# Expert weight pieces in eight lasting places, output weights by column halves, two modulation pieces multiplied ahead of their layer

## The chip, the cores and the metric

One NeuronCore of a Trainium2 chip runs the whole program. The metric is the device time of one execution in microseconds (us). Five engines run side by side and meet through semaphores: TensorE (PE, matmuls), VectorE (DVE), ScalarE (ACT), GpSimd (POOL) and SyncE (SP), whose queue issues nearly all transfers from HBM.

## What is computed

The reference chains a two-layer transformer block with experts and a second, hybrid block. The change touches the first alone. Per layer (512 tokens of width 1024, all float32):

```python
mod = c_act @ w_ada[l] + b_ada[l]                     # 6 x 1024 modulation values
h = rms_norm(x, norm1_g[l]) * (1.0 + scale1) + shift1
proj = h @ w_in[l]                                    # latents, rope part, convolution input
attn_out, conv_out = mla_group(...), conv_group(...)
x = x + gate1 * (concatenate([attn_out, conv_out]) @ w_out[l])
h2 = rms_norm(x, norm2_g[l]) * (1.0 + scale2) + shift2
# 16 experts; each takes the 64 tokens with the highest affinity
hid = silu(xe @ w_gate) * (xe @ w_up)
ye = (hid @ w_down) * gate
x = x + gate2 * scatter(ye)
```

Each expert has three 1024 x 1024 matrices, 12.6 MB, for 64 tokens.

## The kernel before, in words

`prologue` loads x and the constants, turns x, computes the rope tables and stores them to HBM, and issues the loads of the first layer's vector rows (13 small ones) and of modulation pieces 0 to 3. It is a block of its own: all engines meet at its end, before `layer` begins. `layer` is one such block, run twice in a loop over `l`.

Inside `layer` each engine has its own instruction stream; the order of transfers is the order of SP's stream, and a wait in it holds back all that stands behind.

**Start of a layer.** w_ada comes in twelve pieces of 512 columns (2 MB each, `ADA_PLACES` says in which of four places). PE multiplies a piece in `ada_chunk` (L541), 64 matmul records, ACT copies the row out (`ada_kept`, L909), PE turns it (`ada_turn`, L547). Pieces 0 to 3 hold shift1 and scale1, which `h` needs. Piece 0 is followed by the broadcast of 1/rms (L519), from which DVE makes the normalized x (L1101, eight operations); then come pieces 1, 2 and 3, DVE's sum `modulation(0)` (L1107), ACT's h (L933), DVE's low half of the split (L1143) and the first matmul of the input projection (L567). SP begins the layer with the first four tiles of w_in (`load_input`, L147).

**Output weights.** w_out (4 MB) lies in ring parts 3 and 4, split by ACT (L1007) and POOL (L491) during the attention into a high and a low part that are stored in parts 3, 4, 5 and in `one_hot_T`. `out_passes` (L689 to L691) multiplies them, output tile after output tile, and counts `wout_done` up to 8.

**Experts.** The weights of an expert come in six pieces of 2 MB: gate 0, 1, up 2, 3, down 4, 5. There are six lasting places in `ring`, and three `early` places that expert 1's pieces 0 to 2 use once. In `sp`: pieces 0 to 2 of expert 0 are issued when the attention is done, pieces 3 to 5 and the three early ones when all of w_out is used. From then on each piece is issued when PE has used the one that was in its place (`chunk_used`). PE's loop runs over pairs of experts: gate and up (L829), gather for the next expert (L792), turns (L838, L798), gates and a row of ranks (L804, L805), down (L851); every second expert is followed by the scatter of a pair's outputs (L814, L817), which DVE adds into x (L1318). The last pair is scattered behind the loop, where PE first waits for ACT (L1059) and POOL (L497) to split the outputs.

The issue order of the weights of expert e in the loop is

```python
def shifted(e, j):
    sp.wait_ge(chunk_used, 6 * e + (j - 5))
    load(e, j)
```

that is, pieces in the order of their use, each released six pieces ahead of its use. In the first layer the loop's tail loads modulation pieces 0 to 3 of the next layer, in the second the memory and the first weights of the next block (`load_mixer`).

## Time and profile before

| | |
|---|---|
| median of 3 runs | 2645.95 us (2644.2 to 2647.7) |
| the profiled execution | 2650.9 us, its span 2649.2 us |
| PE busy | 2484.0 us, 94% of the span |
| DVE, ACT, POOL busy | 1109.6, 871.3, 294.7 us |
| read from HBM | 641.99 MB |
| layer 0, first matmul of the input projection | at 46.84 us |
| layer 0, experts | from 335.67 to 805.5 us |
| layer 1, experts | from 1130.92 to about 1599.9 us |

Times in a timeline count from the start of the span. The span is one execution, 5 us longer than the median of the runs. Busy matmul time has modelled ends, so a busy PE can still be a PE that waits a little. The idle time in front of an instruction stands in brackets, with what ended it. A transfer has two times: how long SP was held by its issue, and how long it took from issue to landing.

### The profile page before, as it was taken

What the parts mean: (1) busy time and instruction counts of PE and PEld (TensorE: products, weight loads), DVE (VectorE), ACT (ScalarE), POOL (GpSimd) and SP (SyncE); (2) the same over time, 40 slices, a digit from 0 to 9 for tenths busy, and PEclk for the clock granted to TensorE, in tenths of its full rate; (3) what the DMA queues carried; (4) which work ended last, traced back from release to release, by engine and by line L of the source; (5) the groups of instructions that cost most, each with busy time, mean ns of one, the idle gap of its engine ahead of it and who ended that gap; (6) DMA issues with size and microseconds to landing.
All of it is one profiled execution on the core that took longest, in us unless ns stands there. A gap on an engine that the chain in (4) does not pass through costs nothing. (4 is left out here: it accounts for less than half of the span.)

```text
span 2649.2 us, 31866 instructions
## 1 busy us (share of the span) xinstructions
PE 2484.0 (94%) x12913; PEld 1487.9 (56%) x12913; DVE 1109.6 (42%) x1700; ACT 871.3 (33%) x1195; POOL 294.7 (11%) x126
## 2 busy tenths in 40 slices
PE   6989799999997989799999998999999999989998
PEld 5834533333335834533333337887788777756665
DVE  4974322222223974322222225647521112456765
ACT  4246111111114247111111116556532234245553
POOL 0002000000000002000000005000244423200000
PEclk8988899999998988899999999999999999989999
DMA  9700579999999600589999996532223321159995
GB/s 339 275 1 37 221 307 409 410 410 410 410 409 346 244 1 34 221 321 409 410 410 410 410 409 191 168 93 81 79 75 97 131 71 57 48 177 373 358 354 208
DMA packets 276596, 650.49 MB, mean 246 GB/s; under 512 B 12144, under 2 KB 110718, under 8 KB 276222
## 3 DMA queue, kind: packets, MB, share of 16 engines
q1 hardware_dynamic: 273310, 638.87, 64.2%
q0 software_dynamic: 2592, 7.87, 0.8%
q10 hardware_dynamic: 576, 2.10, 0.2%
q8 instruction: 84, 1.38, 0.2%
q14 instruction: 34, 0.28, 0.0%
HBM read 641.99 MB, written 8.39 MB: 246 GB/s over the span
## 5 line engine op out<-in xcount | busy, mean ns | idle before, releaser
L829 PE MATMUL ps<-ring,scr 128*64 128x512 f32 x1952 | 425.3, 593 | 0.8 <-DMA ring<-in_w_up 0.8
L829 PEld LDWEIGHTS ps<-ring,scr 128*64 128x64 f32 x1952 | 138.7, 137 | 277.2 <-issue 274.0
L851 PE MATMUL ps<-ring,scr 128*64 128x512 f32 x1024 | 231.9, 606 | 1.4 <-ACT scr L1047 1.4
L1579 POOL TENSOR_TENSOR raw_r<-raw,w_high 128x2048 fp32r<-128x2048 f32 (+1 forms) x38 | 165.3, 4359 | 460.0 <-ACT w_high L1846 460.0
L1601 PE MATMUL ps<-x_high,w_high 128*128 128x512 f32 x464 | 186.6, 402 | 5.4 <-DVE y L2242 5.4
L1603 PE MATMUL ps<-x_high,raw_r 128*128 128x512 f32 x464 | 184.3, 397 | 0.0
L1602 PE MATMUL ps<-xT_r,w_high 128*128 128x512 f32 x464 | 182.9, 394 | 0.0
L1123 DVE SCALAR_TENSOR_TENSOR one_hot_T<-h_tok,convw,one_hot_T 128x512 f32<-128x512 f32 x240 | 170.5, 763 | 1.8
L497 POOL TENSOR_TENSOR one_hot_T_r<-hy,one_hot_T_r 128x1024 fp32r<-128x1024 f32 x16 | 38.5, 2405 | 1124.0 <-ACT one_hot_T_r L1059 1124.0
L1331 DVE TENSOR_TENSOR scr<-scr,ps 128x512 f32<-128x512 f32 x32 | 22.0, 688 | 312.5 <-PE ps L829 312.5
L2720 DVE TENSOR_TENSOR ring_r<-ring,ring_high 128x2048 fp32r<-128x2048 f32 x56 | 127.6, 2286 | 58.4 <-ACT ring_high L2598 57.9
L851 PEld LDWEIGHTS ps<-ring,scr 128*64 128x64 f32 x1024 | 71.9, 139 | 138.7 <-issue 136.6
L1055 ACT ACTIVATE hy<-ps,gcol 64x512 f32<-64x512 f32 x64 | 43.7, 683 | 285.6 <-PE ps L851 285.2
L1846 ACT ACTIVATE w_high<-raw 128x2048 fp32r<-128x2048 f32 (+1 forms) x58 | 105.9, 1826 | 93.3 <-DMA raw<-in_p_b 49.2
L1318 DVE SCALAR_TENSOR_TENSOR xT<-ps,mod,xT 128x512 f32<-128x512 f32 x128 | 86.5, 744 | 117.3 <-PE ps L817 116.6
L1038 ACT ACTIVATE hy<-ps 128x512 f32<-128x512 f32 x32 | 19.1, 597 | 330.8 <-PE ps L792 330.8
L2598 ACT ACTIVATE ring_high<-ring 128x2048 fp32r<-128x2048 f32 x56 | 107.4, 1917 | 60.5 <-DMA ring<-in_w_up 60.5
L792 PE MATMUL ps<-h_tok,scr 128*64 128x512 f32 x512 | 120.3, 613 | 3.0 <-DVE sel_e L1302 3.0
L2511 PE MATMUL ps<-ring_high,xg_high 128*128 128x512 f32 x224 | 100.8, 450 | 3.5 <-DVE xg_low L2726 3.2
L2545 PE MATMUL ps<-ring,hidT 128*128 128x512 f32 x224 | 101.0, 593 | 2.6 <-ACT hidT L2608 2.6
L1601 PEld LDWEIGHTS ps<-x_high,w_high 128*128 128x128 f32 x464 | 87.6, 189 | 27.3 <-DVE y L2242 5.9
L1311 DVE TENSOR_TENSOR scr<-ps,smod 128x512 f32<-128x512 f32 x32 | 22.1, 692 | 187.3 <-PE ps L798 187.3
(563 smaller groups left out, 4536.2 us busy)
## 6 DMA issues: line engine op xcount, KB each, us to landing
ring<-in_w_down SPq DMA_DIRECT2D x64, 2048.0 KB, 15.2
ring<-in_w_up SPq DMA_DIRECT2D x62, 2048.0 KB, 18.4
ring<-in_w_gate SPq DMA_DIRECT2D x60, 2048.0 KB, 14.9
ring<-in_w_up SPq DMA_DIRECT2D x56, 1024.0 KB, 7.2
ring<-in_w_ada SPq DMA_DIRECT2D x22, 2048.0 KB, 13.2
ring<-in_w_down SPq DMA_DIRECT2D x28, 1024.0 KB, 7.7
raw<-in_w_in SPq DMA_DIRECT2D x24, 1024.0 KB, 5.1
raw<-in_w_in SPq DMA_DIRECT2D x20, 512.0 KB, 5.3
```

The source lines that it names most:

```text
L792: mm = pe.matmul(ps[CAP * half:CAP * (half + 1), 0, :], s_e[:, t, 0:CAP], h_tok3[:, t, half * HALF:(half + 1) * HALF], start=(t == 0), sto ...
L829: mm = pe.matmul(ps[CAP * half:CAP * (half + 1), 1 + j // 2, :], x_e[:, at_x:at_x + CAP], weights[:, k, half * HALF:(half + 1) * HALF], st ...
L851: mm = pe.matmul(ps[CAP * half:CAP * (half + 1), 4, :], hidT[:, at_f:at_f + CAP], weights[:, k, half * HALF:(half + 1) * HALF], start=(j = ...
L1123: op = dve.scalar_tensor_tensor(acc[:, c, :], src, w, acc[:, c, :], ALU.mult, ALU.add)
L1579: pool.tensor_tensor(dst, src, high.bitcast(F32), ALU.subtract).then_inc(w_ready, 1)
L1601: pe.matmul(out, s_high, m_high, start=(n == 0), stop=False)
L1602: pe.matmul(out, s_high, m_low, start=False, stop=False)
L1603: mm = pe.matmul(out, s_low, m_high, start=False, stop=(n == len(terms) - 1))
L1846: act.activation(slot_of(w_high, n), landed_chunk(n), ACT.Copy).then_inc(w_split, 1)
L2545: mm = pe.matmul(ps[:, 2 + half, :], hT[n % 2][:, k, :], w[:, k, half * HALF:(half + 1) * HALF], start=(e == 0 and k == 0), stop=(e == PER ...
L2598: act.activation(high[q], raw[q], ACT.Copy).then_inc(w_split, 1)
L2720: dve.tensor_tensor(low[q], raw[q], high[q].bitcast(F32), ALU.subtract).then_inc(w_ready, 1)
```

## The change

Four things change, all in the first block.

**Pieces.** There are eight lasting places: the six in the ring, and two (`odd`) in `hy` and `one_hot_T` that hold pieces 0 and 1 of the odd experts. Ring places 0 and 1 hold pieces 0 and 1 of the even experts, ring places 2 to 5 pieces 2 to 5 of every expert. A ninth place (`once`) holds piece 2 of expert 1. SP's order in the loop is now, for each expert: pieces 0 and 1 of the *next* expert (`following`), then pieces 2 to 5 of this one (`rest`).

**Output weights.** w_out is loaded, split and multiplied by column halves, not by row halves, so that half of its room is free at `wout_done` 4. The nine first pieces are issued in four steps instead of two: at the end of the attention, when the last of `mix` is split, at `wout_done` 4 and at 8.

**Modulation.** Pieces 0 and 1 of a layer are multiplied before the layer's block begins (`ada_ahead`, into bank 7): those of layer 0 at the end of the prologue, those of layer 1 in the tail of layer 0, in front of the last scatter. `load_input` moves from the start of the layer to the prologue and to the tail of layer 0 as well.

**Ranks.** The selector `sel_e` and a second copy of the ranks (`rank_row`, one more DVE operation) are float32r, so that L805 is a one-pass matmul.

```diff
+def ada_ahead(pe, M, c):
+    for kt in range(KT):
+        for g in range(4):
+            pe.matmul(M["ps"][GROUP * g:GROUP * (g + 1), 7, c * P:(c + 1) * P], c_spread_ahead(M)[:, kt, :], ada_place(M, ADA_PLACES[c])[:, kt, g * P:(g + 1) * P],
+                      start=(kt == 0), stop=(kt == KT - 1))
...
             for c in range(4):
                 load_ada(sp, A, M, 0, c, ahead)
+            load_input(sp, A, M, 0, ahead)
             sp.wait_ge(p_act, 2)
             sp.dma_start(A["rope"], tables).then_inc(ahead["tables"], 16)
...
+            pe.wait_ge(x_kept, KT)
+            pe.wait_ge(p_spread, 1)
+            for c in range(ADA_PRE):
+                pe.wait_ge(ahead["ada"][c], 16)
+                ada_ahead(pe, M, c)
...
-    chunk = [ring[:, i * CHUNK:(i + 1) * CHUNK].rearrange("p (k n) -> p k n", k=4) for i in range(6)]
-
-    early = [x[:, a:a + CHUNK].rearrange("p (k n) -> p k n", k=4) for x, a in ((hy, CHUNK), (one_hot_T, CHUNK), (one_hot_T, 0))]
-    EARLY = len(early)
+    chunk = [ring[:, i * CHUNK:(i + 1) * CHUNK].rearrange("p (k n) -> p k n", k=4) for i in (3, 4, 5, 0, 1, 2)]
+
+    odd = [x[:, a:a + CHUNK].rearrange("p (k n) -> p k n", k=4) for x, a in ((hy, CHUNK), (one_hot_T, 0))]
+    once = one_hot_T[:, CHUNK:2 * CHUNK].rearrange("p (k n) -> p k n", k=4)
...
-            load_input(sp, A, M, l, ahead)
             ada_chunk(4)
...
-            for k in range(0, KT, 4):
-                sp.dma_start(w_out[:, k:k + 4], w[:, k:k + 4]).then_inc(w_out_in, 16)
+            for half in range(2):
+                sp.dma_start(w_out[half], w[:, :, half * HALF:(half + 1) * HALF]).then_inc(w_out_in, 16)
...
-            for j in range(6):
-                if j in (0, 3):
-                    sp.wait_ge(*((pv_done, HEADS) if j == 0 else (wout_done, KT)))
-                load(0, j)
-            for j in range(EARLY):
-                load(1, j)
-            for n in range(6):
-                sp.wait_ge(chunk_used, n + 1)
-                load(1 + (n + EARLY) // 6, (n + EARLY) % 6)
-
+            sp.wait_ge(pv_done, HEADS)
+            for j in (3, 4, 5):
+                load(0, 0, j)
+            sp.wait_ge(mix_split, KT)
+            load(0, 1, 2)
+            sp.wait_ge(wout_done, KT // 2)
+            load(0, 0, 0)
+            load(0, 0, 2)
+            sp.wait_ge(wout_done, KT)
+            load(0, 0, 1)
+            load(0, 1, 0)
+            load(0, 1, 1)
+
+            def following(n, r):
+                for j in range(2):
+                    sp.wait_ge(chunk_used, 12 * n + (6 * r - 6 + j + 1))
+                    load(*((n, 1) if r == 0 else (n + 1, 0)), j)
+
+            def rest(n, r, js):
+                for j in js:
+                    sp.wait_ge(chunk_used, 12 * n + (6 * r - 6 + j + 1))
+                    load(n, r, j)
+
+            for j in range(2):
+                sp.wait_ge(chunk_used, j + 1)
+                load(1, 0, j)
+            rest(0, 1, range(3, 6))
             with sp.If(l < DEPTH - 1):
                 load_rows(sp, A, M, (l + 1) % DEPTH, ahead)
+            following(1, 0)
+            rest(1, 0, (2,))
...
+            with sp.Fori(2, PAIRS - 1) as n:
+                for r in range(2):
+                    following(n, r)
+                    rest(n, r, range(2, 6))
+            following(PAIRS - 1, 0)
+            rest(PAIRS - 1, 0, range(2, 6))
+            rest(PAIRS - 1, 1, range(2, 6))
             with sp.If(l < DEPTH - 1):
...
                 for c in range(3):
-                    sp.wait_ge(chunk_used, used - (5 - c))
+                    sp.wait_ge(chunk_used, 6 * (EXPERTS - (2 if c < 2 else 1)) + c + 1)
                     load_ada(sp, A, M, after, c, ahead)
                 sp.wait_ge(xe_mm, EXPERTS)
                 load_ada(sp, A, M, after, 3, ahead)
+                sp.wait_ge(chunk_used, 6 * EXPERTS)
+                load_input(sp, A, M, after, ahead)
             with sp.If(l > DEPTH - 2):
                 sp.wait_ge(st_mm, EXPERTS)
+                sp.wait_ge(chunk_used, 6 * EXPERTS - 4)
                 load_mixer(sp, A, M, ahead)
...
-                pe.matmul(ps[:, 6, :], sel_e[:], rankm, start=True, stop=True).then_inc(st_mm, 1)
+                pe.matmul(ps[:, 6, :], sel_e[:], rank_row, start=True, stop=True).then_inc(st_mm, 1)
...
+            with pe.If(l < DEPTH - 1):
+                pe.wait_ge(st_free, EXPERTS + 1)
+                pe.wait_ge(c_again, 1)
+                for c in range(ADA_PRE):
+                    pe.wait_ge(ada_in[ADA_PLACES[c]], ada_landed(c, l + 1))
+                    ada_ahead(pe, M, c)
...
             dve.tensor_tensor(rankm, rank, affT, ALU.mult).then_inc(rank_ready, 1)
+            dve.tensor_tensor(rank_row, rank, affT, ALU.mult)
```

## Rows read from the trace of the kernel before

**Rows 1.** The page, costliest groups: busy, mean ns, idle and releaser.

```profile
L829 PE MATMUL ps<-ring,scr 128*64 128x512 f32 x1952 | 425.3, 593 | 0.8 <-DMA ring<-in_w_up 0.8
```

**Rows 2.** Windows, one in layer 0's experts; last columns: clock, DMA share, GB/s.

```profile
700.00:750.00 50.00, 49.67 (x236) 19.51 (x234) 11.38 (x21) 4.32 (x7) 0.00 (x0) 1.00 1.03 410
```

**Rows 3.** Timeline, layer 1, PE at experts 14 and 15.

```profile
1543.55 10.47 PE L829 MATMUL ps<-ring,scr 128*64 128x512 f32 x48
1554.78 3.65 PE L829 MATMUL ps<-ring,scr 128*64 128x512 f32 x16 [0.76 <-DMA ring<-in_w_up]
```

**Rows 4.** Line L442, four single issues: duration in ns, start, time to landing.

```profile
L442 SPq DMA_DIRECT2D ring<-in_w_up x1: 373/373/373, 339.4 to 339.4; - x1
...
DMA to landing us min/median/max: 9.2/9.2/9.2
...
L442 SPq DMA_DIRECT2D ring<-in_w_up x1: 3932/3932/3932, 736.7 to 736.7; - x1
...
DMA to landing us min/median/max: 22.4/22.4/22.4
...
L442 SPq DMA_DIRECT2D ring<-in_w_up x1: 373/373/373, 1134.6 to 1134.6; - x1
...
DMA to landing us min/median/max: 9.0/9.0/9.0
...
L442 SPq DMA_DIRECT2D ring<-in_w_up x1: 4786/4786/4786, 1531.2 to 1531.2; - x1
...
DMA to landing us min/median/max: 23.5/23.5/23.5
```

**Rows 5.** Timeline, PE in layer 0's experts 13 and 14, one slow group of layer 1.

```profile
741.42 1.12 PE L805 MATMUL ps<-krg,sel_e 16*128 16x512 f32 x2
...
743.06 7.09 PE L851 MATMUL ps<-ring,scr 128*64 128x512 f32 x32
749.98 12.61 PE L829 MATMUL ps<-ring,scr 128*64 128x512 f32 x57
...
1297.28 8.78 PE L851 MATMUL ps<-ring,scr 128*64 128x512 f32 x32
```

**Rows 6.** Groups of lines within layer 0's experts: busy, mean ns.

```profile
L1318 DVE SCALAR_TENSOR_TENSOR xT<-ps,mod,xT 128x512 f32<-128x512 f32 x56 | 37.5, 743 | 43.8 <-PE ps L817 43.8
...
L817 PE MATMUL ps<-hy_r,one_hot_T_r 128*128 (+1 forms) x56 | 22.1, 394 | 0.0
```

**Rows 7.** Timeline, SP's issues at the end of the prologue and behind it.

```profile
21.74 5.24 SPq L218 DMA_DIRECT2D rope_tables<-ring  x1
27.68 11.30 SPq L147 DMA_DIRECT2D ring<-in_w_in  x4
```

**Rows 8.** Timeline, start of layer 0 up to the input projection.

```profile
27.75 0.40 PE L534 MATMUL ps<-const,hy 83*128 83x83 f32 x1 [6.31 <-PEq L206]
...
29.01 3.64 PE L541 MATMUL ps<-ring,one_hot_T 128*32 128x128 f32 x64 [0.66 <-DVE one_hot_T L1095]
...
34.66 4.87 DVE L1101 TENSOR_TENSOR hy<-xT,ps 128x512 f32<-128x512 f32 x8 [4.50 <-PE ps L519]
...
43.45 0.17 DVE L1107 TENSOR_TENSOR mod<-ps,vec 128x16 f32<-128x16 f32 x1 [3.91 <-PE ps L547]
...
46.84 0.77 PE L567 MATMUL ps<-hy_r,one_hot_T_r 128*128 128x512 f32 x1 [3.51 <-DVE hy_r L1143]
```

**Rows 9.** Timeline, tail of layer 0 behind the last expert.

```profile
808.02 0.50 PE L814 MATMUL ps<-hy_r,one_hot_T_r 128*128 128x512 f32 x1 [2.56 <-ACT one_hot_T_r L1059]
...
810.52 0.79 PE L817 MATMUL ps<-hy_r,one_hot_T_r 128*128 128x512 f32 x1 [2.00 <-POOL one_hot_T_r L497]
...
811.35 6.44 DVE L1318 SCALAR_TENSOR_TENSOR xT<-ps,mod,xT 128x512 f32<-128x512 f32 x8 [14.45 <-PE ps L817]
```

**Rows 10.** Timeline, POOL's last split of w_out in layer 0.

```profile
226.56 2.35 POOL L491 TENSOR_TENSOR ring_r<-ring,one_hot_T_r 128x1024 fp32r<-128x1024 f32 x1 [1.06 <-ACT one_hot_T_r L1007]
```

**Rows 11.** Timeline, DVE waits for the turned ranks, layer 0.

```profile
325.00 0.23 DVE L1295 COPY rankT<-ps 128x64 f32<-128x64 f32 x1 [0.70 <-PE ps L784]
```

More of the change, by code:

```diff
@@ L361, in layer @@
     sel_e, gcol = M["sel_e"], M["gcol"]
+    rank_row = M["hy_r"][0:EXPERTS, 3 * S:4 * S]
     x_e, sg, hid = scr[:, 0, :], scr[:, 1, :], scr[:, 2, :]
@@ L460, in _ @@
                     sp.dma_start(rowsA[KT * i:KT * (i + 1), :], A[name].rearrange("(k p) -> k p", p=P)).then_inc(mem_in, 16)
-            def shifted(e, j):
-                sp.wait_ge(chunk_used, 6 * e + (j - 5))
-                load(e, j)
-            for j in range(EARLY, 6):
-                shifted(2, j)
-            with sp.Fori(3, EXPERTS) as e:
-                for j in range(6):
-                    shifted(e, j)
+            rest(1, 0, range(3, 6))
+            following(1, 1)
+            rest(1, 1, range(2, 6))
+            with sp.Fori(2, PAIRS - 1) as n:
[5 more added lines that the diff above has]
+            rest(PAIRS - 1, 1, range(2, 6))
             with sp.If(l < DEPTH - 1):
-                after, used = (l + 1) % DEPTH, 6 * EXPERTS
+                after = (l + 1) % DEPTH
                 for c in range(3):
-                    sp.wait_ge(chunk_used, used - (5 - c))
+                    sp.wait_ge(chunk_used, 6 * (EXPERTS - (2 if c < 2 else 1)) + c + 1)
                     load_ada(sp, A, M, after, c, ahead)
@@ L549, in _ @@
             pe.wait_ge(c_spread, 1)
-            ada_chunk(0, 0)
+            ada_chunk(2, 2)
             pe.wait_ge(n_inv, 1)
             pe.wait_ge(vec_ready, 2)
-            broadcast(7, root).then_inc(n_bc, 1)
-            for c in range(1, 4):
-                ada_chunk(c, c)
+            broadcast(3, root).then_inc(n_bc, 1)
+            ada_chunk(3, 1)
             for c in range(4):
@@ L687, in out_passes @@
             def out_passes(dt, n, kt, first, last):
-                tile = slice(dt * P, (dt + 1) * P)
-                pe.matmul(ps[:, dt, :], w_out_high[kt][:, tile], mix_high[:, kt, :], start=first, stop=False)
-                pe.matmul(ps[:, dt, :], w_out_high[kt][:, tile], mix_low[:, kt, :], start=False, stop=False)
-                return pe.matmul(ps[:, dt, :], w_out_low[:, kt, tile], mix_high[:, kt, :], start=False, stop=last)
+                half, tile = dt // 4, slice((dt % 4) * P, (dt % 4 + 1) * P)
+                high, low = w_out_high[half][:, kt, tile], w_out_low[half][:, kt, tile]
+                pe.matmul(ps[:, dt, :], high, mix_high[:, kt, :], start=first, stop=False)
+                pe.matmul(ps[:, dt, :], high, mix_low[:, kt, :], start=False, stop=False)
+                return pe.matmul(ps[:, dt, :], low, mix_high[:, kt, :], start=False, stop=last)
             def early_output(n):
                 kt = MIX_ORDER[n]
-                pe.wait_ge(w_out_ready, kt + 1)
+                pe.wait_ge(w_out_ready, 4 * (EARLY_OUT // 4) + kt // 2 + 1)
                 pe.wait_ge(mix_ready, n + 1)
@@ L817, in scatter, with expert @@
                     pe.matmul(ps[:, bank, :], ye_lo[:, tile], one_hot, start=False, stop=True).then_inc(out_done, 1)
-            def expert(e, last, scattered=None):
+            def expert(n, r, last, scattered=None):
+                e = 2 * n + r
                 pe.wait_ge(xe_ready, e + 1)
@@ L823, in expert @@
                 for j in range(4):
-                    weights, landed, count = expert_chunk(e, j)
+                    weights, landed, count = expert_chunk(n, r, j)
                     pe.wait_ge(landed, count)
@@ L845, in expert @@
                 for j in range(4, 6):
-                    weights, landed, count = expert_chunk(e, j)
+                    weights, landed, count = expert_chunk(n, r, j)
                     pe.wait_ge(landed, count)
@@ L923, in w_in_split_tile @@
                                    w_in[i].unsqueeze(2).to_broadcast([P, KT, 2, ROPE]), ACT.Copy).then_inc(w_in_split, 1)
-            for c in range(3):
-                ada_kept(c, c)
+            for c in range(ADA_PRE):
+                ada_kept(c, 7, c * P)
             for i in range(2):
                 w_in_split_tile(i)
-            ada_kept(3, 3)
+            ada_kept(2, 2)
+            ada_kept(3, 1)
             act.wait_ge(mod_ready, 1)
```

90 lines of the change are left out of this document (51 added, 39 removed).

## The prediction, made before the change was run

> **What bounds the kernel now.** I read the page first, then the windows by stage, then the timeline of one pair of experts, and last the landing times of single weight pieces. PE is busy 94% of the span, and in the expert stage, 470 us in each layer, it does not stop: the weight matmuls had 0.8 us of idle time in front of them in the whole program [rows 1]. But the same stage moves 410 GB/s with the DMA engines at a share of 1.03 [rows 2]: the transfers are saturated too. A piece of 2 MB (2.097 MB) then takes 2.097 / 410 = 5.12 us.
>
> So two limits stand side by side. The reader should ask which of them has slack, and look at a piece that is used late. Take piece 3 of expert 14. In layer 0 it is issued at 736.7 and lands 22.4 later, at 759.1 [rows 4]; expert 14 begins at 749.98 [rows 5], and the three pieces before it take 10.3 (10.47 with the modelled end [rows 3]), so it is needed at 760.3: 1.2 us of slack are left. In layer 1 it is issued at 1531.2, lands at 1554.7 [rows 4], and PE waits 0.76 us for it [rows 3]. An early piece lands 9 us after its issue, these ones 22 to 24: the queue has grown through the loop. The transfers are a little slower than PE, and the loop ends just as the stock is used up. PE saved in the loop is worth nothing unless the pieces land sooner, and what decides is when piece 3 of expert 14 lands.
>
> **The expert loop.** What the change does to PE: L805 goes from a float32 matmul of 1.12 us [rows 5] to a one-pass one, 0.39 us [rows 6]: 0.73 less for each expert, 11 us in a layer if PE alone set the time. At worst it brings nothing.
>
> What it does to the pieces: I number the issues. Before, issues are in order of use, so piece j of expert e is number 6e + j + 1, and piece 3 of expert 14 is number 88. After, the loop issues pieces 0 and 1 of the next expert ahead of pieces 2 to 5 of this one. The first nine are the stock, then come 2.0, 2.1, 1.3, 1.4, 1.5, 3.0, 3.1, 2.2 and so on (expert.piece): piece 3 of expert 14 is number 90. Its place is released by the same event as before (expert 13's piece 3 used), but two pieces that nobody needs for another expert stand ahead of it in a first in, first out queue. The two additional places therefore hold pieces 0 and 1 longer and give pieces 2 and 3 nothing.
>
> Against that the queue starts fuller. Before, issues 10 to 15 are released by expert 0, and then nothing is issued for expert 1's first three pieces, which came from the early places, so the DMA engines fall idle. Number 10 landed at 339.4 + 9.2 = 348.6 [rows 4]; 78 pieces of 5.12 on, number 88 would have landed at 748.0, and it landed at 759.1: 11.1 us of idle transfers. After, number 10 is issued at the same event; the only gap that I find is in front of expert 1's piece 4, which waits for expert 0's piece 4 while nothing else is queued: about 3.5 us. Number 90 lands at 348.6 + 80 x 5.12 + 3.5 = 761.7, and the 13 small rows, which before fell into the idle time, add perhaps 0.4: 762.1. PE needs it at 760.3 or, with the cheaper L805, sooner; so PE waits, and passes this point 1.8 us later than before. Behind it only one L805 is left that is cheaper (0.73), and expert 15's pieces 2 to 5 are numbers 93 to 96 in either order and land early. Experts of layer 0: +1.1 us. Bounds: -2 (no gap, 3.5 less, one more late release less) and +3.
>
> Layer 1 has also the memory load (1 MB, 2.6 us of transfer), which before fell into the idle time. Number 10 at 1134.6 + 9.0 = 1143.6 [rows 4], number 90 at 1143.6 + 409.6 + 3.5 + 2.6 = 1559.3 against 1554.7 before: +4.6, less 0.73: +3.9. Bounds: 0 and +6.
>
> The nine first pieces now spread over the output projection and land some 15 us earlier; expert 0 begins at 335.67 either way, since PE comes from the routing, so this is worth nothing. The column halves: ACT and POOL make the same eight operations, the last of POOL's ending at 228.9 [rows 10], with the attention still running, and it is this cover that makes them cost nothing. The additional DVE operation `rank_row` (16 x 512, about 0.7 us) falls into the 0.70 us in which DVE waits for the turned ranks [rows 11]; nothing, 0.7 at worst in each layer. The new wait in front of `load_mixer` holds only transfers that queue behind the last pieces anyhow.
>
> **Start of layer 0.** The prologue is a block, and PE's first instruction behind it (27.75) was released by the block's end, after 6.31 us of idle time [rows 8]. What ended last in it was SP: the issue of the rope tables held SP from 21.74 to 26.98 [rows 7]. A queue full of modulation pieces holds SP back. The four w_in tiles behind the block held it for 11.30 us more, to 38.98 [rows 7]. The change moves these four into the prologue, ahead of the rope tables. The same five transfers go through the same full queue: SP's last issue in the prologue ends between 38.3 (the 0.7 us between the blocks saved) and 40.6 (one more of the last wait); I take 39.5. All engines begin the layer 12.5 us later.
>
> What the layer then saves: two pieces of L541 at 3.64 us [rows 8] and less. But they are not all on the path. Piece 0 was followed by the broadcast, and DVE's eight operations ended at 34.66 + 4.87 = 39.5, that is 11.8 behind the first transpose; the sum for the modulation came at 43.45, 15.7 behind it [rows 8]. After, piece 2 stands where piece 0 stood, only piece 3 follows the broadcast, and DVE's eight operations end last: the sum comes at 11.8, 3.9 sooner. From there it is 3.4 to the first projection matmul, as now (43.45 to 46.84). Start of layer 0: +12.5 - 3.9 = +8.6. The input projection keeps PE busy from there, so this is carried to the end. Bounds: -2.2 (SP not held, below) and +10.
>
> By the Trainium skill, DMA: Bandwidth & Descriptors, section "Issuing engines are not separate DMA queues", the time that an issue costs its sequencer is usually small against the transfer. The rows here show 5.24 us for the issue of a 0.5 MB transfer, against it; by that rule the block would end when PE does and the sum would be about -1.9 us (rival 1).
>
> **Tail of layer 0 and start of layer 1.** PE was idle 2.56 us for ACT's split and 2.00 for POOL's in front of the last scatter [rows 9]. The two pieces now lie there: modulation piece 1 is number 98 and lands at about 348.6 + 88 x 5.12 + 4 = 803, before expert 15 ends (806.6 by the above). At full clock they take some 3.7 us, under the 5.0 in which the scatter's second matmul waits for POOL anyway; nothing, and 3.7 us if the pieces land late. PE is not idle there any more, so its clock should stay up: DVE's additions would take 5.4 instead of 6.44 us, -1.0 (56 of them took 37.5 us, eight 5.4 [rows 6, 9]). The next layer's start then saves the same 3.9 us. SP ends its issues, four w_in tiles too, at about 816, before PE ends its sums. Together -4.9; bounds -6 and -1.
>
> **Sum.** +8.6 + 1.1 - 4.9 + 3.9 = +8.7 us. The profiled execution took 2650.9 (span 2649.2 and 1.7 around it), so 2659.6 on its terms; the runs' median stands 5 us lower: 2645.95 + 8.7 = 2654.7 us.
>
> **The rivals.**
> 1. *SP is not held in the prologue.* Each issue costs 0.4 us, as the 373 ns ones do [rows 4], and the block ends with PE: 21.44 (27.75 - 6.31) and two pieces of 3.64, 28.7 instead of 27.0. Layer 0: +1.7 - 3.9 = -2.2; sum -2.2 + 1.1 - 4.9 + 3.9 = -2.1, 2643.9 us. For it: a small transfer in front of w_in let the first of them through. Against: 11.30 us for four issues. Chance 0.14.
> 2. *The two places carry the loop (faster).* If the pieces that are used next still land in time, PE runs without a wait and L805's 0.73 counts 15 times in each layer: 8.6 - 11.0 - 4.9 - 11.0 - 0.8 = -19.1, 2626.9 us. It decides from the point where number 90 lands by 749 in layer 0. For it: all pieces of a layer are in some 8 us sooner than before. Against: the count of the queue. Chance 0.11.
> 3. *Waits lower the clock.* PE now waits for pieces 2 and 3 in the later pairs. A stretch at half clock made one L851 group 8.78 us long instead of 7.09 [rows 5], 1.7 each. A pair has 61.4 us by the transfers and 58 by PE, so most of it is absorbed; if half of some 16 waits cost it, +14: 2668.7 us. The Trainium skill, TensorE: Matmul & The Clock Gate, section "HAM oscillation — how this bites in real kernels", describes this: waits for transfers in a loop put the array back to its lower clock each time; no row here shows such a wait. Chance 0.09.
>
> **How the numbers follow.** The forecast as summed has 0.62, the rivals 0.14, 0.11 and 0.09, 0.04 is none of these. Its own range is 2649 to 2661. The range 2643 to 2664 takes in rival 1 and leaves out rival 2 and most of rival 3. 0.2% is 5.3 us, about what a measurement of this kernel can tell from no change: faster is below 2640.7, slower above 2651.2. Faster: rival 2 and a little of rival 1, 0.14. Same: most of rival 1 and the forecast's lower edge, 0.24. Slower: 0.62.
>
> **What would show it.** The first transpose of layer 0 (L534 before) at about 40 us, released by the prologue's end, with SP's issues up to there, and the first projection matmul at 55.5. In the loop, idle time of PE in front of pieces 2 and 3 that a DMA ended, over 8 us in each layer, while L805 takes 0.4. Piece 3 of expert 14 landing 413 us behind the tenth issue's landing. The experts of layer 0 lasting 471 us, those of layer 1 473. Layer 1's first projection matmul 14.7 to 15.5 us behind its first transpose. I am wrong if the prologue ends before 32 us, or if PE shows no wait for weights.

## The result: about 0.6% slower

| | before | after |
|---|---|---|
| median of 7 runs | 2645.95 us | 2664.26 us |
| lowest and highest | 2641.8 and 2654.4 | 2655.6 and 2669.9 |
| the profiled execution's span | 2649.2 us | 2665.9 us |

The ratio is 1.0061, with a 95% interval of 1.0038 to 1.0083: on 2646 us that is 16 us more, 10 to 22. Forecast were 2654.7 us, 8.7 more. So the direction was right and the size about half of the measured one. By the ratio the time is 2662 us, 1 us above the forecast's own range (2649 to 2661) and inside the wider one, which ends at 2664; the median itself lies on that edge.

The 16.7 us between the two profiled spans, by stage ("experts" is from expert 0's first matmul to the end of expert 15's last down matmul):

| stage | before | after | difference | forecast |
|---|---|---|---|---|
| up to layer 0's first projection matmul | 46.8 | 54.3 | +7.4 | +8.6 |
| from there to expert 0 | 288.8 | 287.9 | -0.9 | 0 |
| experts of layer 0 | 469.8 | 472.0 | +2.2 | +1.1 |
| to layer 1's first projection matmul | 37.0 | 35.0 | -2.0 | -4.9 |
| from there to expert 0 | 288.5 | 288.2 | -0.2 | 0 |
| experts of layer 1 | 469.1 | 474.0 | +4.9 | +3.9 |
| behind the last expert | 1049.2 | 1054.6 | +5.4 | 0 |

### The profile page after: what moved, and what is told of

It is laid out like the page before. It is cut to its first block and busy times, and to the rows that moved or that the text cites. A ratio compares the mean times of both kernels' runs of the same rounds, so it can differ in the third digit from the quotient of the medians.

```text
span 2665.9 us, 31788 instructions
## 1 busy us (share of the span) xinstructions
PE 2465.4 (92%) x12881; PEld 1482.7 (56%) x12881; DVE 1107.9 (42%) x1704; ACT 871.4 (33%) x1195; POOL 292.6 (11%) x126
## 5 line engine op out<-in xcount | busy, mean ns | idle before, releaser
L879 PE MATMUL ps<-ring,scr 128*64 128x512 f32 x1504 | 332.8, 594 | 27.9 <-DMA ring<-in_w_up 27.3
L879 PEld LDWEIGHTS ps<-ring,scr 128*64 128x64 f32 x1504 | 106.0, 137 | 248.6 <-issue 201.6
L901 PE MATMUL ps<-ring,scr 128*64 128x512 f32 x1024 | 226.8, 595 | 1.4 <-ACT scr L1105 1.4
L901 PEld LDWEIGHTS ps<-ring,scr 128*64 128x64 f32 x1024 | 70.7, 137 | 134.8 <-issue 133.0
L1663 PEld LDWEIGHTS ps<-x_high,w_high 128*128 128x128 f32 x464 | 87.7, 189 | 27.5 <-DVE y L2304 5.9
L1664 PEld LDWEIGHTS ps<-xT_r,w_high 128*128 128x128 f32 x464 | 87.6, 189 | 22.8 <-issue 2.2
```

Of the source, the lines that this page charges most:

```text
L879: mm = pe.matmul(ps[CAP * half:CAP * (half + 1), 1 + j // 2, :], x_e[:, at_x:at_x + CAP], weights[:, k, half * HALF:(half + 1) * HALF], st ...
L901: mm = pe.matmul(ps[CAP * half:CAP * (half + 1), 4, :], hidT[:, at_f:at_f + CAP], weights[:, k, half * HALF:(half + 1) * HALF], start=(j = ...
L1663: pe.matmul(out, s_high, m_high, start=(n == 0), stop=False)
L1664: pe.matmul(out, s_high, m_low, start=False, stop=False)
```

## The profile after

The timeline of SP, and then of PE and DVE, at the start of layer 0. Columns: start, duration, engine, line, operation; in brackets the idle time and what ended it.

```profile
21.56 16.25 SPq L163 DMA_DIRECT2D ring<-in_w_in  x4
37.86 1.68 SPq L235 DMA_DIRECT2D rope_tables<-ring  x1
```

```profile
25.30 1.95 PE L127 MATMUL ps<-ring,one_hot_T 128*32 128x128 f32 x64 [0.56 <-DMA ring<-in_w_ada]
40.31 0.40 PE L582 MATMUL ps<-const,hy 83*128 83x83 f32 x1 [13.05 <-PEq L222]
...
44.91 1.16 PE L567 MATMUL ps<-krg,const 128*128 128x128 f32 x8
...
54.27 0.77 PE L614 MATMUL ps<-hy_r,one_hot_T_r 128*128 128x512 f32 x1 [5.20 <-DVE hy_r L1201]
```

```profile
46.10 4.87 DVE L1159 TENSOR_TENSOR hy<-xT,ps 128x512 f32<-128x512 f32 x8 [3.39 <-PE ps L567]
50.89 0.16 DVE L1165 TENSOR_TENSOR mod<-ps,vec 128x16 f32<-128x16 f32 x1
```

PE has multiplied both pieces by 27.3 and then stands still for 13.05 us, until SP has got rid of its issues (37.86 + 1.68 = 39.54). The four w_in tiles held SP for 16.25 us here against 11.30 in [rows 7]; the first transpose comes at 40.31 against 27.75 in [rows 8].

In the expert stage the page's group of gate and up matmuls shows the new waits (in [rows 1] it was 0.8 us), and the timeline of layer 0's expert 12 shows two of them, in front of pieces 2 and 3:

```profile
L879 PE MATMUL ps<-ring,scr 128*64 128x512 f32 x1504 | 332.8, 594 | 27.9 <-DMA ring<-in_w_up 27.3
```

```profile
702.99 3.65 PE L879 MATMUL ps<-ring,scr 128*64 128x512 f32 x16 [1.37 <-DMA ring<-in_w_up]
708.11 3.65 PE L879 MATMUL ps<-ring,scr 128*64 128x512 f32 x16 [1.47 <-DMA ring<-in_w_up]
...
748.09 0.50 PE L854 MATMUL ps<-hy_r,sel_e 16*128 16x512 f32 x1
```

The matmul of the rank row takes 0.50 us where it took 1.12 [rows 5]; PE's time saved stands in front of the pieces. The issue of the tenth piece in layer 0 and that of piece 3 of expert 14 (number 90), by line, in two stretches:

```profile
L467 SPq DMA_DIRECT2D ring<-in_w_gate x1: 372/372/372, 346.0 to 346.0; - x1
...
DMA to landing us min/median/max: 9.2/9.2/9.2
```

```profile
L467 SPq DMA_DIRECT2D ring<-in_w_up x2: 4928/5010/5091, 740.7 to 745.8; - x2
...
DMA to landing us min/median/max: 23.7/23.7/23.7
```

Landings at 355.2 and 769.5: 414.3 us apart, where the count of the queue gave 413.1. In layer 1 it is 416.8 us against 415.7. And the tail of layer 0:

```profile
814.09 3.70 PE L127 MATMUL ps<-ring,one_hot_T 128*32 128x128 f32 x128
817.72 0.51 PE L863 MATMUL ps<-hy_r,one_hot_T_r 128*128 128x512 f32 x1
819.25 0.51 PE L866 MATMUL ps<-hy_r,one_hot_T_r 128*128 128x512 f32 x1 [1.02 <-POOL one_hot_T_r L545]
...
823.90 1.52 PE L561 MATMUL ps<-hy,ones 128*32 128x128 f32 x48
828.58 0.65 PE L561 MATMUL ps<-hy,ones 128*32 128x128 f32 x16 [3.16 <-issue]
834.82 0.40 PE L582 MATMUL ps<-const,hy 83*128 83x83 f32 x1 [5.60 <-issue]
...
849.13 0.77 PE L614 MATMUL ps<-hy_r,one_hot_T_r 128*128 128x512 f32 x1 [5.60 <-DVE hy_r L1201]
```

The two pieces do lie in the time in which PE waited for ACT and POOL [rows 9]. But the sums stop for 3.16 us with nothing waited for. The DMA view of that stretch (825.5 to 827.5) shows what arrived in it: one packet of instructions, beside data transfers at 99% of the DMA engines' time.

```profile
q1 hardware_dynamic: 1081, 0.55, 99.4%
q8 instruction: 1, 0.02, 3.7%
```

## The experiments

All stages in one table; the ratio is to runs of the kernel before on the same chip (their medians lay between 2644.4 and 2649.1 us), so compare ratios first. "Start" is layer 0's first projection matmul; "turn" is from layer 0's last down matmul to layer 1's first projection matmul; "waits" are PE's for weight pieces in layer 0.

| run | start | experts 0 | experts 1 | waits | turn | median us | ratio, 95% |
|---|---|---|---|---|---|---|---|
| before | 46.8 | 469.8 | 469.1 | 0.0 | 37.0 | 2645.95 | 1 |
| after | 54.3 | 472.0 | 474.0 | 12.8 | 35.0 | 2664.26 | 1.0038 to 1.0083 |
| e1 input at layer 0 | 46.7 | 472.5 | 473.7 | 13.3 | 34.2 | 2653.14 | 1.0015 to 1.0042 |
| e2 order of use | 53.5 | 462.1 | 463.6 | 4.4 | 41.1 | 2649.18 | 1.0000 to 1.0030 |
| e3 rank f32 | 54.5 | 476.4 | 474.9 | 4.3 | 30.8 | 2671.92 | 1.0086 to 1.0121 |
| e4 order, rank f32 | 54.0 | 468.1 | 468.1 | 0.0 | 41.7 | 2660.85 | 1.0034 to 1.0074 |
| f1 order, no ahead | 46.4 | 463.5 | 463.7 | 4.3 | 40.4 | 2634.68 | 0.9945 to 0.9975 |
| f2 before, rank one-pass | 46.2 | 467.3 | 467.0 | 8.9 | 39.8 | 2640.68 | 0.9959 to 0.9993 |
| f3 input at both starts | 46.6 | 472.1 | 475.2 | 12.8 | 33.9 | 2650.77 | 1.0010 to 1.0037 |
| f4 no ahead | 46.2 | 471.9 | 473.7 | 12.9 | 35.5 | 2653.64 | 1.0015 to 1.0050 |
| g1 order, ahead | 46.4 | 462.2 | 463.6 | 4.3 | 40.9 | 2641.66 | 0.9961 to 0.9994 |
| g2 order from first | 46.7 | 472.3 | 474.0 | 13.0 | 37.4 | 2656.53 | 1.0019 to 1.0057 |
| g3 first pieces late | 46.4 | 462.1 | 463.6 | 4.4 | 37.5 | 2639.25 | 0.9941 to 0.9985 |
| h1 changed again | 53.8 | 472.5 | 473.8 | 13.3 | 34.7 | 2664.13 | 1.0033 to 1.0075 |

### e1: the w_in tiles of layer 0 back at the start of the layer

```diff
             for c in range(4):
                 load_ada(sp, A, M, 0, c, ahead)
-            load_input(sp, A, M, 0, ahead)
...
+            with sp.If(l < 1):
+                load_input(sp, A, M, 0, ahead)
             ada_chunk(4)
```

> The changed kernel, with the four w_in tiles of layer 0 issued at the start of layer 0 again and not in the prologue. My theory (the prologue's end waits for SP, whose issues a full queue holds back): the prologue ends when the rope issue and PE's two modulation pieces end, both at about 27.2 us, the first transpose of layer 0 comes at 28 to 29 us instead of 40.3, and the first projection matmul at 44 to 47 us instead of 54.3, since the w_in tiles still land at 38 to 44 us; 7 to 10 us less in all, carried to the end. Rival 1 (moving the issues is free either way): the first projection matmul stays at 53 to 55 us. The rest of the kernel keeps its stages: experts 472.0 and 474.0 us.

The timelines of PE and of SP in this run:

```profile
24.48 3.36 PE L127 MATMUL ps<-ring,one_hot_T 128*32 128x128 f32 x64 [2.26 <-DMA ring<-in_w_ada]
28.62 0.29 PE L583 MATMUL ps<-const,hy 83*128 83x83 f32 x1 [0.79 <-PEq L222]
...
35.57 3.35 PE L590 MATMUL ps<-h_tok,one_hot_T 128*32 128x128 f32 x64 [2.42 <-DMA h_tok<-in_w_ada]
...
42.49 0.69 PE L596 MATMUL ps<-const,one_hot_T 128*128 128x128 f32 x2 [3.21 <-ACT one_hot_T L967]
46.69 0.77 PE L615 MATMUL ps<-hy_r,one_hot_T_r 128*128 128x512 f32 x1 [3.51 <-DVE hy_r L1202]
```

```profile
20.54 5.84 SPq L234 DMA_DIRECT2D rope_tables<-ring  x1
28.33 9.91 SPq L163 DMA_DIRECT2D ring<-in_w_in  x4
```

The four issues are held here too, for 9.91 us, but behind the block's end, where nobody waits for SP. The idle 13.05 us become 0.79 and the start is 7.6 us shorter; rival 1 falls. The start is also no better than before (46.8), although two pieces less stand in it. PE waits 2.42 us for piece 3, but is through with it at 38.92; what ends last is ACT. In its stream the splits of two w_in tiles stand in front of the copies of pieces 2 and 3, and ACT waits for the tiles until 40.27:

```profile
40.27 2.00 ACT L978 ACTIVATE one_hot_T_r<-ring 128x1024 fp32r<-128x1024 f32 x2 [10.05 <-DMA ring<-in_w_in]
42.18 0.42 ACT L967 ACTIVATE one_hot_T<-ps 128x128 f32<-128x128 f32 x2
```

In the kernel before the same wait ends at 40.78, there in front of piece 3's copy:

```profile
40.78 2.00 ACT L920 ACTIVATE one_hot_T_r<-ring 128x1024 fp32r<-128x1024 f32 x2 [2.19 <-DMA ring<-in_w_in]
```

So the landing of w_in sets the start of layer 0 in both, and the pieces ahead are worth nothing there.

### e2, e3 and e4: issue order and rank matmul, each alone and both

The order turned from expert 6 on (e2, e4):

```diff
-            with sp.Fori(2, PAIRS - 1) as n:
+            for r in range(2):
+                following(2, r)
+                rest(2, r, range(2, 6))
+            with sp.Fori(3, PAIRS - 1) as n:
                 for r in range(2):
-                    following(n, r)
                     rest(n, r, range(2, 6))
-            following(PAIRS - 1, 0)
+                    following(n, r)
             rest(PAIRS - 1, 0, range(2, 6))
+            following(PAIRS - 1, 0)
```

and the rank matmul in float32 again (e3, e4; `sel_e` is float32 with it and `rank_row` is left out):

```diff
-                pe.matmul(ps[:, 6, :], sel_e[:], rank_row, start=True, stop=True).then_inc(st_mm, 1)
+                pe.matmul(ps[:, 6, :], sel_e[:], rankm, start=True, stop=True).then_inc(st_mm, 1)
```

> The changed kernel, with the issue order of the expert loop turned from expert 6 on: pieces 2 to 5 of this expert go first, then pieces 0 and 1 of the next. My theory (first in, first out queue at its full rate; two pieces that nobody needs yet stand ahead of the urgent ones): piece 3 of expert 14 is number 88 again with only 3.5 us of gap, PE waits 2 to 6 us in a layer instead of about 12 to 16, and L854's saving comes through: experts of layer 0 462 to 464 us instead of 472.0, of layer 1 464 to 466 instead of 474.0; the whole 16 to 20 us less. Rival (the transfers bind whatever their order, since PE saved has nowhere to come from): both stages within 2 us of the changed kernel's. Rival (the waits come from less room for the pieces and not from the order): no more than 3 us less in each layer.

> The changed kernel, with L854 a float32 matmul of 1.1 us again (and without the second copy of the ranks). My theory (in the changed order the pieces bind, so PE's time is covered by its waits): experts of layer 0 at most 2 us longer than 472.0 and of layer 1 at most 2 us longer than 474.0, with PE's waits for weights down from about 13 us to under 4 in layer 0. Rival 2 (PE binds and L854 saves its 0.73 us each time): 9 to 11 us longer in each layer.

> Both edits: order of use from expert 6 on, and L854 in float32 again. My theory: PE binds and hardly waits; experts of layer 0 469 to 471 us, of layer 1 468 to 471, so that L854 is worth 6 to 9 us a layer in this order (against the run with the order alone) and under 2 in the other. Rival (the transfers bind whatever their order): no difference between the two runs with the new order.

The group of gate and up matmuls between 300 and 900 us, in the kernel after, e2, e3 and e4 (last column: idle time and what ended it):

```profile
L879 PE MATMUL ps<-ring,scr 128*64 128x512 f32 x752 | 166.3, 594 | 13.1 <-DMA ring<-in_w_up 12.8 <-DVE scr L1372 0.3
```

```profile
L882 PE MATMUL ps<-ring,scr 128*64 128x512 f32 x752 | 164.8, 593 | 4.7 <-DMA ring<-in_w_up 4.4 <-DVE scr L1375 0.3
```

```profile
L879 PE MATMUL ps<-ring,scr 128*64 128x512 f32 x752 | 168.0, 601 | 4.4 <-DMA ring<-in_w_up 4.3
```

```profile
L882 PE MATMUL ps<-ring,scr 128*64 128x512 f32 x752 | 164.1, 592 | 0.0
```

The order alone takes 9.9 and 10.4 us off the two stages: 462.1 and 463.6, inside the 462 to 464 and a hair below the 464 to 466 that were expected. No place and no byte was added, so the waits came from the two pieces in front of the urgent ones, and the rivals (any order binds; too little room) fall. In e2 piece 3 of expert 14, number 88 again, lands 404.6 us behind the tenth against 414.3. The float32 rank matmul makes the stages 6.0 and 4.5 us longer with this order (e4 against e2) and 4.4 and 1.0 without (e3 against after, where I had said at most 2). Nowhere in these four is it all of 15 x 0.62 = 9.3 us: what PE saves comes back as waits, 8.5 us of them more in the kernel after than in e3, 4.4 more in e2 than in e4. But 4.4 and 8.5 are more than 9.3 together, and the rest is the clock. In e3's layer 0 the granted clock was 0.57 from 336 to 344 us, at the first expert, and at half once more for 3.4 us, with PE busy throughout (last columns: clock, DMA share, GB/s):

```profile
500.00:512.00 12.00, 12.00 (x54) 4.79 (x52) 2.07 (x3) 1.17 (x2) 0.00 (x0) 0.86 1.03 410
```

The weight matmuls take 3.7 us more there than in e3's layer 1. Taken off, this leaves about 1 us for the rank matmul in this order, as expected; an estimate, since waits can take up a part of the time lost. Each stage of e4 has one such stretch too (1.7 us), so the 6 us that were expected as the least in the turned order are reached in layer 0 only with the clock's part, and layer 1's 4.5 falls short. e4's layer 0 came 0.9 us below the expected 469 to 471, its layer 1 inside 468 to 471.

What I had not expected is e2's turn: 41.1 us instead of 35.0. The timeline of PE at its last down matmul's end:

```profile
805.28 1.95 PE L127 MATMUL ps<-ring,one_hot_T 128*32 128x128 f32 x64 [1.77 <-DMA ring<-in_w_ada]
810.65 2.64 PE L127 MATMUL ps<-ring,one_hot_T 128*32 128x128 f32 x64 [3.42 <-DMA ring<-in_w_ada]
```

The loop ends 10 us sooner, but the stream of transfers doesn't: modulation pieces 0 and 1 land at 805 and 811 us in either kernel, and PE now waits 5.2 us for them in front of the last scatter. A stop in the sums, as in the kernel after, is in it too (3.81 us). So the next runs took the modulation part out.

### f1 and f4: nothing multiplied ahead, with the new order and without

f4 is the changed kernel without `ada_ahead` and with `load_input` at each layer's start, that is the modulation of the kernel before; f1 has the turned order as well.

> The changed kernel with the order of use from expert 6 on, and with the modulation and the w_in loads as in the kernel before (nothing multiplied ahead, load_input at the start of each layer). My theory: the start of layer 0 is that of before (first projection matmul 46.8 us), the experts take 462 to 464 us in both layers, and the 5.2 us in which PE waited for modulation pieces 0 and 1 in the tail of layer 0 (seen with the new order) are gone: 18 to 19 us from the last down matmul to the first transpose. In all 12 to 14 us less than the kernel before, 2631 to 2635 us. Rival (the stream of transfers binds across the layer's end as well): the pieces behind the experts land when they did, the first projection matmul of layer 1 comes no more than 1 us sooner than with the order alone measured from the start of the experts (503.2 us), and the gain is under 8 us.

> The changed kernel, with the whole modulation part undone: nothing multiplied ahead, load_input at the start of each layer. What is left of the change are the places, their order, the column halves and the ranks. My theory: the first projection matmul of layer 0 at 46.8 us, the tail of layer 0 18.6 us, the start of layer 1 18.4 us, and the experts as in the changed kernel, 472 and 474 us; 7 us more than before in all, that is 0.3% slower or the same. Rival (the start and the tail are worth what the change meant, so undoing them costs): longer than the changed kernel.

f4 leaves places, order, column halves and ranks: the experts stay at 471.9 and 473.7, the start goes back to 46.2. Undoing the modulation part gives 8.1 us at the start and costs 0.5 in the turn, so the rival (start and tail gain by the change) falls; without the stop of 3.16 us the turn of the kernel after would have been 3.7 us shorter than f4's, still less than the start loses. f1 has the lowest median of the study, 0.4% under the kernel before (0.25 to 0.55%; g3's interval overlaps). Its 2634.7 us lie in the expected 2631 to 2635, though the gain by the ratio is 10.6 us and not 12 to 14: the kernel before ran at 2644.4 on this chip. Its turn was 40.4 instead of the expected 37: the stop in the sums came up here too, with nothing multiplied ahead and no w_in tile in the queue:

```profile
806.53 1.72 PE L555 MATMUL ps<-hy,ones 128*32 128x128 f32 x50
811.56 0.64 PE L555 MATMUL ps<-hy,ones 128*32 128x128 f32 x14 [3.32 <-issue]
```

From the start of the experts to layer 1's projection it took 503.9 us against e2's 503.2, so the rival's first sign came true. Its second, a gain under 8 us, is left open by an interval of 6.6 to 14.5. Without the stops (3.32 and 3.81) it would be 500.6 against 499.4: this pair does not show that taking the waits out gained anything, and what f1 gains over e2 is the start.

### f2: the kernel before with the one-pass rank matmul alone

Beside the lines below `sel_e` is float32r.

```diff
-                pe.matmul(ps[:, 6, :], sel_e[:], rankm, start=True, stop=True).then_inc(st_mm, 1)
+                pe.matmul(ps[:, 6, :], sel_e[:], rank_row, start=True, stop=True).then_inc(st_mm, 1)
...
             dve.tensor_tensor(rankm, rank, affT, ALU.mult).then_inc(rank_ready, 1)
+            dve.tensor_tensor(rank_row, rank, affT, ALU.mult)
```

> The kernel before, with L805 as a one-pass matmul and the second copy of the ranks, and nothing else. My theory (six places in order of use, 11 us of idle transfers at the loop's start, the stock used up at its end): PE then waits for pieces 2 and 3 in the last pairs and keeps only a part of the 11 us: experts of both layers 465 to 467 us instead of 469.8 and 469.1, waits of 6 to 9 us each. Rival 2 (PE alone sets the time): 458 to 460 us. Rival (nothing is left, the transfers bind): 469 us.

467.3 and 467.0 us, waits of 8.9 and 8.5 (expected were 465 to 467 and 6 to 9): the stages are 2.5 and 2.1 us shorter, about a quarter of the saving, and the rest is waited away. The rank matmul's own part may be less, since the stages of the kernel before have two and one stretches of 3.4 us at half clock (1.7 us each) and those of f2 none. The edit alone makes the kernel before 0.24% faster (0.07 to 0.41%). Of the change's four parts this one was a gain, and the parts around it lost more.

### f3: w_in at both layers' starts, the pieces still ahead

> The changed kernel, with load_input at the start of both layers; the two modulation pieces stay ahead. It tests the tail of layer 0, where the sums of the changed kernel stop for 3.2 us with nothing waited for. Theory A (PE's instructions are fetched behind the w_in transfers, which lie in the queue then): the 3.2 us shrink to under 1, and the last down matmul is 17 to 18.5 us before the first transpose instead of 20.7. Theory B (the fetch falls there because 256 more instructions stand in front of it): a gap of 2 to 4 us stays. Start of layer 0 as in the run with the input at layer 0: first projection matmul at 46 to 47.5 us.

The stop is 1.62 us here: neither theory's number. With the other runs it shows more. The stop was 3.2 us in after and again in h1, 3.0 in e1, 3.8 in e2 and f2, 5.0 in e4, 3.3 in f1, 3.9 in g1, and absent in before, e3, f4, g2 and g3. e3 has both the pieces ahead and the w_in tiles and no stop; f1 and f2 have neither and have it. So neither part is needed for it, and neither brings it each time. They may still make it likelier: after, h1, e1, e2, f3 and g1 have the same PE code and all six stop, f1, f4, g2 and g3 share theirs and one of the four does.

What PE waits for can be read from the instruction packets in the traces. In all nine a packet of 16 KB arrived between the beginning and the end of the sums, and they went on 1.3 to 1.5 us behind its end (in after it ended at 827.26, the sums went on at 828.58). In the other five the last such packet had ended at least some 0.6 us before the sums began (f4's next one came in their last 0.7 us, without a stop). That speaks for a wait for instructions, though no run moved the packet; why it is late in some executions was not found. Where there is no stop, the pieces ahead shorten the way from the last down matmul to the first transpose from 18.6 (before) to 17.2 (e3), 1.4 us.

### g1, g2 and g3

g1 keeps the modulation part and has both mends, the turned order and e1's. g2 is f1 in order of use from the loop's first piece on, g3 is f1 with the first pieces issued as late as before:

```diff
+            rest(0, 1, range(3, 6))
             for j in range(2):
                 sp.wait_ge(chunk_used, j + 1)
                 load(1, 0, j)
-            rest(0, 1, range(3, 6))
```

```diff
-            sp.wait_ge(mix_split, KT)
-            load(0, 1, 2)
-            sp.wait_ge(wout_done, KT // 2)
-            load(0, 0, 0)
-            load(0, 0, 2)
             sp.wait_ge(wout_done, KT)
-            load(0, 0, 1)
-            load(0, 1, 0)
-            load(0, 1, 1)
+            load(0, 0, 0)
+            load(0, 0, 1)
+            load(0, 0, 2)
+            load(0, 1, 0)
+            load(0, 1, 1)
+            load(0, 1, 2)
```

> The changed kernel with both mends that keep the modulation part: order of use from expert 6 on, and the w_in tiles of layer 0 issued at the start of layer 0. Against the run with the new order and nothing multiplied ahead it tells what the two pieces ahead are worth. My theory: with the faster loop pieces 0 and 1 land at about 805 and 811 us, 3 to 8 us behind the last down matmul, so PE waits for them about as long as the next start saves: from the last down matmul of layer 0 to layer 1's first projection matmul 40 to 42 us, against 40.4 there; the first projection matmul of layer 0 at 46 to 47 us; median within 3 us of 2634.7. Rival (the pieces ahead are worth the 4 us of the start): 36 to 37 us from the last down matmul to the projection, and a median 4 us lower.

> The run with the new order and nothing multiplied ahead, but in order of use from the first piece of the loop: expert 1's pieces 3 to 5 go ahead of expert 2's pieces 0 and 1, and so on. My theory (the queue must not fall idle early, and must not carry early pieces ahead of urgent ones late; the transfers lost in the first experts are missing in the last): PE waits again 11 to 17 us in each layer, and the experts take 471 to 474 us in both, as long as in the changed kernel. Rival (order of use is the better order wherever it stands): 464 us or less in both.

> The run with the new order and nothing multiplied ahead, but with six of the nine first pieces issued only when all of w_out is used, as in the kernel before, in order of use. It undoes what the column halves made room for. My theory (PE comes from the routing, and number 10 is issued at the same event either way): no difference, experts 463 to 465 us in both layers and expert 0 starting 9 us after the first gather. Rival (the early spread starts the stream earlier and feeds the loop): experts 2 to 10 us longer.

g1: 40.9 us from the last down matmul to the projection, 40.4 in f1, each with such a stop (3.88 and 3.32); PE waits for the second piece as in e2:

```profile
799.57 3.15 PE L127 MATMUL ps<-ring,one_hot_T 128*32 128x128 f32 x64 [3.46 <-DMA ring<-in_w_ada]
```

What the next start saves is waited away (the rival had 36 to 37 us), and no gain shows in the medians either: 2641.7 against 2634.7, where I had expected 3 us at most between them. The intervals of the ratios overlap, so that g1 is slower isn't shown.

g2 uses f1's places with, behind the first nine pieces, the order of use of the kernel before, and loses all that the turned order gave: 472.3 and 474.0, the 471 to 474 that were expected. SP's timeline shows why:

```profile
341.22 0.37 SPq L460 DMA_DIRECT2D ring<-in_w_up  x1
350.63 3.80 SPq L460 DMA_DIRECT2D ring<-in_w_down  x2
```

Expert 0 begins at 327.2, and SP stands in front of piece 3 of expert 1 until 341.2, 14 us, with two free places behind it in its stream; in the kernel after this took 3.8 (342.2 to 346.0). Number 88 lands 427.7 us behind expert 0's start, number 90 of the kernel after 427.4, number 88 of e2 417.5. What the first experts leave idle is missing in the last.

g3: 462.1 and 463.6, no difference to g1's 462.2 and 463.6. f1, from which it differs only in this, had 463.5 and 463.7; the first 3 us of its layer 0's experts ran at half clock. The room that the column halves make is worth nothing, as forecast.

### h1: the changed kernel again

> The changed kernel once more, unedited, to tell what repeats. My theory (5.4 of the 16.7 us between the two profiles lie behind the experts of layer 1, in code that the change does not touch, and vary from execution to execution, like the 195 to 202 us from the first projection matmul to the first matmul of the output projection): the first projection matmul of layer 0 comes at 53.5 to 54.5 us and the experts take 472 and 474 us again, within 0.5; the stretch behind the last down matmul of layer 1 takes anything from 1049 to 1057 us. Rival (the change lengthens the second block): it takes 1054 to 1055 us again. Rival for the stop in the sums of layer 0's tail (it belongs to the change): 3 us again; mine: between 0 and 4.

Start 53.8, experts 472.5 and 473.8: these repeat, and so does the stop in the sums (3.17 us), which decides nothing between its rival (3 us again) and my 0 to 4. But this execution's span is 2649.3 us, 16.6 less than the first, and the difference lies elsewhere: from the first projection matmul to the first of the output projection it takes 195.8 us in both layers against 201.7 and 202.0, and behind the last expert 1052.0 against 1054.6. The rival (the change lengthens the second block) wanted 1054 to 1055 again; and f2, which has the second block of the kernel before untouched, took 1054.0 against 1049.2. The windows from 60 to 240 us, first execution and this one (the column before the last two is the granted clock):

```profile
60.00:240.00 180.00, 169.53 (x1103) 101.81 (x1101) 137.06 (x218) 78.76 (x132) 19.09 (x8) 0.93 0.33 116
```

```profile
60.00:240.00 180.00, 169.23 (x1116) 102.87 (x1114) 138.19 (x220) 82.57 (x139) 19.11 (x8) 0.95 0.33 114
```

The clock granted in the attention differs from execution to execution. Over all the runs this stretch took 194.9 to 202.5 us, and the part behind the experts, whose engines have the same work in all, 1049.2 to 1056.8. A single profiled span says nothing on 0.5%; stages do.

## Why the prediction was right, and where it was off

**Start of layer 0** (+8.6 forecast, +7.4). The mechanism and its size held: the prologue ended with SP's held issues, the first transpose came 12.6 us later (12.5 forecast), and e1 took it back. The term for what the layer then saves was 3.9 and measured 5.1. The prediction did not name ACT's wait for w_in, which ends last in the kernel before; e1 shows that without w_in moved up the pieces ahead save nothing. The rest of the difference: DVE's sum came 10.6 us behind the first transpose and not 11.8, since the piece took 3.41 instead of 3.64 us and the eight broadcast matmuls 1.16 instead of 2.04. That is the clock and not the change: granted were 0.93 in the window from 44 to 48 us, against 0.50 from 30 to 34 before. By the rule weighed there (the Trainium skill, DMA: Bandwidth & Descriptors, section "Issuing engines are not separate DMA queues") the issue would have cost little. The trace does not agree: four issues held SP 16.25 us. Rival 1, whose sum the prediction gives once as -1.9 and once as -2.1 (its terms add up to -2.1), falls with it.

**Experts of layer 0** (+1.1, measured +2.2) **and of layer 1** (+3.9, +4.9). The count of the queue was right to 1.2 us in 413, and the waits stood where forecast, 12.8 us in front of up pieces. The rank matmul saves 0.62 us and not 0.73. What the sum of these stages could not hold is that the kernel before spent 3.4 and 1.7 us of them to half clock, the kernel after nothing; what that is worth under the waits no run tells. e2 and g2 show both halves of the count, the two pieces in front and the idle transfers at the start. Rival 2 (the places carry the loop) needed number 90 by 749, that is 413.3 us behind expert 0's start; it came 427.4 behind it, at 769.5.

**Tail of layer 0 and start of layer 1** (-4.9, measured -2.0). The pieces hid behind ACT and POOL, as said, and from the last down matmul to the beginning of the sums it took 9.7 us instead of 11.3: -1.5 where I had -1.0. DVE's additions took 5.36 instead of 6.44 us, at a granted clock of 1.00 where the kernel before had 0.52. The start saved 4.1 (3.9 forecast). What I had not was the stop of 3.16 us. The change is not needed for it, but whether it makes it likelier is open.

**Rival 3** (waits lower the clock) did not come. The half clock came where PE hardly waited. Behind the first 6 us of the experts it stands in five of the six stages with the float32 rank matmul (before, e3, e4), 3.4 us each time and with PE busy before and in it. It stands in none of the 22 stages with the one-pass matmul. More waits are not the reason, since e2 and g1 wait for no piece before 686 us, and the first half-clock stretch of the kernel before is at 502. Why it goes with the float32 matmul was not tested. The windows of the whole stage show it granted in full with 12.8 us of waits in it, each 1.5 us or less; the half clock in the Trainium skill's TensorE: Matmul & The Clock Gate, section "HAM oscillation — how this bites in real kernels", is not seen with waits of this size:

```profile
343.00:814.00 471.00, 454.41 (x2145) 172.83 (x2141) 112.13 (x208) 55.67 (x84) 16.92 (x7) 1.00 1.01 401
```

**The sum.** The four terms measure 7.4 + 2.2 - 2.0 + 4.9 = +12.5 us (in h1 7.0 + 2.7 - 2.4 + 4.7 = +12.0) against +8.7: 1 us more on each expert stage and 2.9 in the turn, less 1.2 at the start. The measured ratio is 16 us, 10 to 22, and in h1 14, 9 to 20, so both sums lie inside. The 5.4 us behind the last expert were 2.8 in h1. Whether the change makes the slower executions of the attention and of the second block likelier (several of its variants have medians some 4 us above their stages' sum) stays open. e3 is the extreme: 27.5 us by the ratio, 13.9 by its stages, whose profile is of its lowest run (2652.8 us, the other four 2670.7 to 2673.2).

## To carry to other kernels

Number the issues: in a first in, first out queue at its full rate a piece's landing is its number times 5.12 us, and a place more helps only if its transfer doesn't go ahead of a more urgent one; while the queue would fall idle, issue whatever is free, and turn to the order of use once it is full. Don't put issues into a full queue just ahead of a point where all engines meet. And where PE is made faster in a loop whose transfers have 1 us of slack, look for what comes due next behind the loop: here the modulation pieces.

## What was not expected of the hardware

- PE can stop for 1.6 to 5.0 us in straight code, with nothing waited for that the profile names: it was so in nine of fourteen profiled executions, each time until 1.3 to 1.5 us behind the end of a 16 KB instruction packet. What makes the packet late was not found. By the Trainium skill, Runtime: NRT & Kernel Launch, section "Instruction fetch mechanics", instructions arrive in blocks of 16 KB and the cost of crossing into the next is mostly hidden; the size agrees with the packet, the cost of 3.16 us does not. That the full queue delays the packet was only argued.
- Unchanged code took 195 to 202 us in different executions; the two shown, 195.8 and 201.7 us, had a granted clock of 0.95 and 0.93 from 60 to 240 us: up to 7 us in each layer, as much as the largest term of this change.
